# One region for the kernel's front: set-up, memory keys, input projection, low-rank products and memory attention joined to the scan

## The reference, cut to what matters

```python
kv = rms_norm(mem, mem_norm_g) @ w_mem_kv          # mem: 256 x 1024, kv: 256 x 512
k_mem, v_mem = kv halves, 4 heads of 64            # k_mem normalised per head
h = rms_norm(x, norm_mix_g[0])
z = h @ rw_in                                      # 1024 x 2816: r, k, v, wa, g, q_mem
z[..., :2560] += rw_mu * (shift_by_one_token(z) - z)
w = sigmoid(w0 + tanh(wa_1) @ rw_w2);  a = sigmoid(a0 + wa_2 @ rw_a2)   # low-rank products
y = the RWKV-7 recurrence of r, k, v, w, a, 12 heads, in chunks of 64 tokens
mix = (group_norm(y) + bonus) * (sigmoid(g) @ rw_g2)
mem_out = softmax(norm(q_mem) @ norm(k_mem).T / 8) @ v_mem
x = x + concat([mix, mem_out]) @ w_out
```

## Time and profile before

| | us |
|---|---|
| three runs | 2153.62, 2156.22, 2162.27 |
| their median | 2156.22 |
| profiled execution, time | 2156.99 |
| profiled execution, span | 2154.8 |
| PE busy in the span | 1994.3 |
| DVE, ACT, POOL busy | 904.5, 733.1, 227.4 |
| mean granted TensorE clock | 0.948 |

### The profile page before, as it was taken

One profiled execution on the slowest core, in us unless ns is written; L12 is line 12 of the kernel. 1 busy time (PEld: TensorE's weight loads), 2 busy tenths in 40 slices (PEclk: granted clock), 3 DMA queues, 4 the chain that ended last, 5 costly groups with the idle time before them and its releaser, 6 DMA issues. The chain is left out here.

```text
span 2154.8 us, 32963 instructions
## 1 busy us (share of the span) xinstructions
PE 1994.3 (93%) x13832; PEld 1598.5 (74%) x13832; DVE 904.5 (42%) x1331; ACT 733.1 (34%) x1221; POOL 227.4 (11%) x308
## 2 busy tenths in 40 slices
PE   5897798857999999999799989999999999999998
PEld 4585577724788888888676558888888988888887
DVE  3442576443443344443214664534332345333223
ACT  4323444233332133222215664422222344222222
POOL 2000566201000000010012320000031000000000
PEclk8898899977999999999958999999999999999999
DMA  4132000000333223362400001332232212233231
GB/s 158 59 97 86 3 3 4 3 8 0 98 98 98 87 90 98 98 133 85 116 2 1 1 1 61 97 98 89 88 101 95 79 40 85 92 98 93 81 95 64
DMA packets 152708, 149.81 MB, mean 70 GB/s; under 512 B 11612, under 2 KB 150010, under 8 KB 152570
## 3 DMA queue, kind: packets, MB, share of 16 engines
q1 hardware_dynamic: 152112, 147.66, 22.3%
q10 hardware_dynamic: 458, 0.12, 0.0%
HBM read 144.62 MB, written 2.10 MB: 68 GB/s over the span
## 5 line engine op out<-in xcount | busy, mean ns | idle before, releaser
L242 DVE TENSOR_TENSOR weight_low<-weight_ring,weight_high 128x2048 fp32r<-128x2048 f32 (+3 forms) x142 | 302.5, 2131 | 495.3 <-ACT weight_high L233 495.2
L233 ACT CAST weight_high<-weight_ring 128x2048 fp32r<-128x2048 f32 (+3 forms) x142 | 251.4, 1771 | 420.6 <-PE psum L262 419.8
L260 PE MATMUL psum<-tail_operand_high,weight_high 128*128 128x512 f32 (+1 forms) x768 | 292.4, 381 | 6.1 <-DVE tail_operand_low L2695 5.4
L262 PE MATMUL psum<-tail_operand_high,weight_low 128*128 128x512 f32 (+1 forms) x768 | 290.1, 378 | 0.0
L261 PE MATMUL psum<-tail_operand_low,weight_high 128*128 128x512 f32 (+1 forms) x768 | 290.1, 378 | 0.0
L260 PE MATMUL psum<-tail_hidden_high,weight_high 128*128 128x512 f32 (+1 forms) x520 | 183.3, 353 | 2.5 <-DVE tail_hidden_low L3141 2.5
L261 PE MATMUL psum<-tail_hidden_low,weight_high 128*128 128x512 f32 (+1 forms) x520 | 182.8, 351 | 0.0
L262 PE MATMUL psum<-tail_hidden_high,weight_low 128*128 128x512 f32 (+1 forms) x520 | 182.6, 351 | 0.0
L260 PEld LDWEIGHTS psum<-tail_operand_high,weight_high 128*128 128x128 f32 x768 | 145.2, 189 | 37.7 <-DVE tail_operand_low L2695 4.8
L261 PEld LDWEIGHTS psum<-tail_operand_low,weight_high 128*128 128x128 f32 x768 | 145.2, 189 | 29.7 <-issue 0.5
L262 PEld LDWEIGHTS psum<-tail_operand_high,weight_low 128*128 128x128 f32 x768 | 145.2, 189 | 29.4
(11 more groups left out here) (405 smaller groups left out, 3191.0 us busy)
## 6 DMA issues: line engine op xcount, KB each, us to landing
weight_ring<-in_w_ff SPq DMA_DIRECT2D x32, 1024.0 KB, 5.2
weight_ring<-in_ffn_w_gate SPq DMA_DIRECT2D x22, 1024.0 KB, 5.3
weight_ring<-in_ffn_w_up SPq DMA_DIRECT2D x22, 1024.0 KB, 5.4
weight_ring<-in_ffn_w_down SPq DMA_DIRECT2D x16, 768.0 KB, 4.6
weight_ring<-in_rw_in SPq DMA_DIRECT2D x11, 1024.0 KB, 5.3
weight_ring<-in_ffn_w_down SPq DMA_DIRECT2D x16, 640.0 KB, 4.2
weight_ring<-in_attn_w_in SPq DMA_DIRECT2D x9, 1024.0 KB, 5.4
weight_ring<-in_w_out SPq DMA_DIRECT2D x4, 1024.0 KB, 5.3
```

Of the source, the lines that this page charges most:

```text
L233: act.copy(self.w_hi[:, slot, 0:n], self.ring[:, slot, 0:n]).then_inc(self.panel_high, 1)
L242: dve.tensor_tensor(self.w_lo[:, slot, 0:n], self.ring[:, slot, 0:n], self.w_hi[:, slot, 0:n], ALU.subtract).then_inc(self.panel_low, 1)
L260: pe.matmul(out, w_hi, x_hi, start=start, stop=False)
L262: return pe.matmul(out, w_lo, x_hi, start=False, stop=stop)
```

## The change

Set-up, the two statistics, the memory keys, the input projection, the low-rank products, memory attention and the preparation of pair 0 become one function, `front`, in one region, and the scan's main part is emitted into the same region.

- 13 panels in another order: q_mem, then wa and g, then the two memory panels, then r, k and v in turns. `front` multiplies 26 groups (two to a panel), numbered s = 0 to 25, in three PSUM banks in turn. Groups 4 to 7 are the memory's and have 256 columns. Groups 8 to 25 are r, k and v (`first_r` is 8).
- The norms of x and mem are taken by token before the transposes: ACT squares a tile of 128 tokens with an accumulated sum, then logarithm and exponential of one column; DVE scales the tile. The gain is applied as the operand is split out of PSUM, by ACT (`mul`) and DVE. x unscaled is turned once more for the residual, two blocks behind each of the groups 2 to 5.
- Behind the groups stand fillers: memory transposes after 1, head sums of q after 3, of k after 6, low-rank products after 8, 9 and 10, scores after 11, 13, 15 and 17, transposes of the weights after 13, 15, 17 and 19, products with `v_mem` after 14, 16, 18 and 20.
- The preparation of pair 0 is spread over the groups 18 to 24.
- SP issues x, panel 0, seven vectors, mem, panel 1, the other vectors and the low-rank weights, then the panels as slots come free. ACT issues eight vectors. The shifts write the slab directly. The low-rank products take half the rows instead of a weight padded with zeros.
- Memory attention's result goes into the slab's place of q_mem, and ACT copies it into `mix` at the start of `rwkv_out`. The region `memory_attention` is gone.

The core of the diff (the functions of the scan's preparation are moved out of the region's bodies and otherwise the same):

```diff
+FRONT = (("rw", 10), ("rw", 9), ("mem", 0), ("mem", 1)) + tuple(("rw", 3 * n + i) for i in range(3) for n in range(3))
...
+    @block.sync
+    def _(sp):
+        for i in range(TT):
+            sp.dma_start(t.x_in[:, i, :], ins["x"][0, i * P:(i + 1) * P, :]).then_inc(x_landed[i], 16)
+        k.load_panels(sp, 1)
+        for dst, src in rows_a[8:]:
+            sp.dma_start(dst, src).then_inc(rows_landed, 16)
+        for i in range(2):
+            sp.dma_start(t.mem_in[:, i, :], ins["mem"][0, i * P:(i + 1) * P, :]).then_inc(mem_landed[i], 16)
+        k.load_panels(sp, 2)
+        for dst, src in rows_rest:
+            sp.dma_start(dst, src).then_inc(rest_landed, 16)
+        for half, name in enumerate(("rw_w2", "rw_a2")):
+            sp.dma_start(t.low[half * HD:(half + 1) * HD, :], ins[name][0]).then_inc(low_landed, 16)
+        k.load_panels(sp, k.lookahead("front"))
...
+    @block.scalar
...
+        for s, (kind, b) in enumerate(groups):
+            bank = ps[:, s % 3, :]
+            group_done(act, s)
...
+                act.copy(t.z[:, c % 2, 1:T + 1], bank).then_inc(evicted, 1)
+            if s % 2:
+                k.split_high(act, 0, 0, s // 2 + 2)
...
+            if first_r <= s < first_r + 3:
+                rates(2 * (s - first_r), 2 * (s - first_r) + 1)
...
+            if s in turn_at:
...
+                act.copy(t.probs_T, ps[:, 6:8, :]).then_inc(copied, 1)
+            if s in scores_at:
...
+                for q in range(TT):
+                    act.activation(t.probs[:, q, :], ps[:, 4 + q // 2, (q % 2) * M:(q % 2 + 1) * M], ACT.Exp,
...
+            if s == 20:
...
+                scan.square(act, 0)
+                scan.still(act, 0)
+            if s == 21:
+                scan.root(act, 0)
+            if s == 22:
+                scan.decays(act, 0)
...
+    @block.vector
...
+        for s, (kind, b) in enumerate(groups):
+            if s % 2:
+                k.split_low(dve, 0, 0, s // 2 + 2)
...
+                dve.wait_ge(evicted, s + 1)
...
+                dve.tensor_tensor(here, z[:, 0:T], z[:, 1:T + 1], ALU.subtract).then_inc(stepped, 1)
...
+            if s == 21:
+                scan.clip(dve, 0)
+            if s == 22:
+                scan.unit_key(dve, 0)
+            if s == 23:
+                scan.against(dve, 0)
+            if s == 24:
+                scan.bonus(dve, 0)
...
+    @block.tensor
...
+        for s, (kind, b) in enumerate(groups):
+            m = s % 2
+            if m == 0:
+                w_hi, w_lo = k.panel(pe, 0, s // 8, s // 2 % 4, KT, PW)
+            if s >= 3:
+                pe.wait_ge(evicted, s - 2)
...
+            if s == 20:
+                pe.wait_ge(copied, heads)
+                scan.key_norm(pe, 0)
+            if s == 22:
+                scan.bonus_sum(pe, 0)
+        pe.wait_ge(placed, heads)
...
+                act.copy(out[:, PAIRS:KT, :], slab[:, SLAB_Q:SLAB_Q + 2, :])
...
-        memory_attention(k, slab, mix)
```

More of the change, by code:

```diff
@@ L11 @@
+from collections import namedtuple
 from contextlib import ExitStack
@@ L143, in add @@
             self.phases.append((name, n, view, kind))
-        add("mem_kv", 2, columns(ins["w_mem_kv"]))
-        add("rw_in", 11, columns(ins["rw_in"][0]))
+        sources = {"rw": columns(ins["rw_in"][0]), "mem": columns(ins["w_mem_kv"])}
+        add("front", len(FRONT), listed([sources[kind](i) for kind, i in FRONT]), "listed")
         add("w_out", 4, columns(ins["w_out"][0]))
@@ L609, in wait_block @@
-def wait_block(eng, k, g0, made, i, b):
-    if b % 2 == 0:
-        eng.wait_ge(made, 4 * i + b // 2 + 1)
-    else:
-        eng.wait_ge(k.panel_used, 4 * i + (g0 + b // 2 + 1))
-def stream_columns(pe, k, name, x, made, bank_free, need=lambda b: b + 1):
-    g0, ps = k.first_panel[name], k.ps
-    n = next(p[1] for p in k.phases if p[0] == name)
-    def body(i, j):
-        w_hi, w_lo = k.panel(pe, g0, i, j, KT, PW)
-        for m in range(2):
-            pe.wait_ge(bank_free, 8 * i + need(2 * j + m))
-            at = slice(m * P, (m + 1) * P)
-            for kt in range(KT):
-                if isinstance(i, int) and i == j == m == 0:
-                    x.ready(pe, kt)
-                last = product(pe, ps[:, 2 * j + m, :], (w_hi[:, kt, at], w_lo[:, kt, at]), x.halves(kt), kt == 0, kt == KT - 1)
-            last.then_inc(k.panel_used if m else made, 1)
-    in_fours(pe, n, body)
@@ new lines, in vector_rows @@
+def vector_rows(k, t):
+    ins, out_a, out_b, out_pe = k.ins, [], [], []
+    for table, tile, row, out in ((VEC_A, t.vec_a, ROW_A, out_a), (VEC_B, t.vec_b, ROW_B, out_b)):
+        for name, n in table:
+            a = ins[name]
+            if n == 1:
+                out += [(tile[row[name]:row[name] + 1, half * HD:(half + 1) * HD], a) for half in range(2)]
+                continue
+            order = {1: "(r c) -> r c", 2: "l (r c) -> (l r) c", 3: "l n (r c) -> (l n r) c"}
+            if name == "rw_r_k":
+                flat = a.rearrange("l (r h) c -> (l r) (h c)", h=2)
+            else:
+                flat = a.rearrange(order[len(a.shape)], c=P)
+            out.append((tile[row[name]:row[name] + n, :], flat))
+    for kv in range(2):
+        for half in range(2):
+            out_pe.append((t.pe_in[:, kv, half * HD:(half + 1) * HD], ins["nsa_cmp_pe_2"][0, kv]))
+    return out_a, out_b + out_pe
```

1611 lines of the change are left out of this document (793 added, 818 removed).

## The result

| | before | after |
|---|---|---|
| median of the timed runs | 2158.23 us (4 runs, 2153.62 to 2162.27) | 2077.84 us (4 runs, 2073.89 to 2079.68) |
| the profiled execution | 2156.99 us, span 2154.8 | 2079.68 us, span 2077.9 |
| mean granted clock of TensorE | 0.948 | 0.965 |
| ratio | | 0.9632, interval 0.9618 to 0.9646 |

The change takes 80.4 us off the median, 3.7%. The forecast was 2077, in a range of 2063 to 2093.

What follows compares the result with a forecast made beforehand. All stages in one were taken as bound by chains of small work, only the projection by PE. Savings of 50.2 (memory attention) and 33.1 (front), less 3.2 returned, gave 80.1 off 2156.99: 2077 us, range 2063 to 2093.

Steps and rivals of the forecast that it cites:

- wait for the memory's low parts: Groups 1 to 7: the residual's first transposes wait 1.2 us for the low parts, ready 8.7 after group 1.
- head 0 waits: Memory attention's first head inside the groups: PE comes after 13.1, its chain ends at 13.9, wait 0.8 us; others none.
- wait in group 22: PE's `bonus_sum` behind group 22 waits 6.2 us for `rk`, held up by the order of ACT's and DVE's queues.
- slow clock behind it: After the pause in group 22 PE's clock falls; 2.6 us taken, between nothing and 5.6.
- scan's first product: End of the front: the scan's first product starts at 203.7 instead of 236.8, minus 33.1 us.
- scan's first product to pair 0's copy (DVE late): Scan start: group 25's split and shift delay DVE's mask operations; 3.2 us comes back, bounds 0 and 6.
- memory attention gone: Behind the scan: the next stage needs only `mix`, so it starts where memory attention did, minus 50.2 us.
- In the loop itself nothing changes, nor behind it: Scan loop and all stages after it: no change in time, so no term in the sum.
- 1.28 for each 128x1024 operation: Front's start: DVE's scaling of x tiles 2 and 3 at two-input speed, last tile ready at 15.3 us.
- the covered late waits: Rival: ACT evicts group 22 early and DVE is free at scan start; 6.2 + 2.6 + 3.2 fall away, 2065; chance 0.12.
- The heads did not wait: Rival denied here: with 5 us more per chain, all four heads wait 2.4 and restarts cost 2.6, 2097; chance 0.22.
- The low clock in the front: Rival: PE's clock stays low through groups 1 to 25 and fillers, 150 us more, 2227; chance 0.02.

Runs made afterwards that it cites:

- kept busy: The kernel after, with seven unused fp32 products of 512 columns on PE ahead of the preparation's second sum behind group 22; 2077.85 us, ratio 0.9623.
- sum later: The kernel after, with PE issuing the preparation's second sum one group later, behind group 23 instead of 22; 2068.95 us, ratio 0.9592.
- split later: The kernel after, with ACT's and DVE's split of the panel behind the projection's last moved from group 25 to the scan's last pair; 2073.82 us, ratio 0.9610.
- no heads: The kernel after, with memory attention's four heads left out on all engines and the normed queries in their place; 2053.89 us.
- rows first: The kernel after, with the seven small rows issued ahead of the first weight panel on the sync queue; 2075.90 us, ratio 0.9623.

## Why the prediction was right, and where not

Step by step, forecast against the profile of after, and against the means of three profiles of each kernel where they matter:

| step | forecast | profiled pair | means of three |
|---|---|---|---|
| group 0 ends | 25.2 | 24.9 | |
| group 7 ends, evicted | 62.6 | 62.4 | |
| wait for the memory's low parts | 1.2 | 0.6 | |
| head 0 waits | 0.8 | 0.3 | |
| wait in group 22 | 6.2 | 6.9 | |
| slow clock behind it | 2.6 | | 2.7 (kept busy) |
| scan's first product | -33.1 | -34.8 | -32.8 |
| scan's first product to pair 0's copy (DVE late) | +3.2 | +3.1 | +3.6 |
| pair 0's copy to pair 5's copy | 0 | +3.2 | +3.1 |
| pair 5's copy to what follows `rwkv_out` | 0 | -2.9 | -2.0 |
| memory attention gone | -50.2 | -50.2 | -53.6 |
| behind the cast | 0 | +4.7 | +2.8 |
| sum, by the span | -80.1 | -76.9 | -78.9 |

The copy is ACT's into `scan_a_av`, one in each pair. What follows `rwkv_out` is memory attention in before and the cast in after.

The mechanism was right at each place that was named: the groups pass at the full clock, each chain lies under them, one pause stands in group 22, and DVE is late for the scan. Sum later, kept busy, split later and no heads each take one of these terms out and find its size, at the scan's first product or (split later) at the cast, within 1 us of the forecast, but for the heads' 1.9.

That the total came out within 1 us is luck, however: wrong terms of 2 to 3.4 us cancelled. "In the loop itself nothing changes, nor behind it" was costed at exactly zero. True of the instructions, it is wrong of the time at three places. First, the loop. The first and last of the six copies, before and then after:
```profile
248.94 0.62 ACT L897 COPY scan_a_av<-scan_tok 128x512 f32<-128x512 f32 x1
...
400.11 0.62 ACT L897 COPY scan_a_av<-scan_tok 128x512 f32<-128x512 f32 x1
```
```profile
217.18 0.62 ACT L1093 COPY scan_a_av<-scan_tok 128x512 f32<-128x512 f32 x1
...
371.56 0.62 ACT L1093 COPY scan_a_av<-scan_tok 128x512 f32<-128x512 f32 x1
```
That is 151.2 against 154.4; the three profiles of each kernel have 150.8 to 151.2 and 153.5 to 154.4. Second, between the last copy and the end of `rwkv_out`, 2.0 come back. Third, a sparse stage far behind, the pool mixer, took 61 to 67 us, at different granted clocks. And the 50.2 of memory attention was read from one execution, at a clock of 0.67; two others had 0.62 and 0.50 and took 53.0 and 57.6. By the mean of three the part taken out was worth 3.4 more than the row said. The last two should have had bounds of some 5 us of their own; the range had room for them, though nothing in it was set aside.

Of the 4.8 that come back between the scan's first product and the cast, split later shows 3.5, at its start. The loop is no shorter in it (154.4), so the loop's 3.1 have another cause. It is not the clock (1.00 in the loop in both kernels), nor PE's work (135.9 busy against 135.3). It is where PE stands still and waits for nothing that the profile shows ("issue"): between the two copies 2.9 to 3.3 in all in the profiles of before, 5.3 to 5.9 in those of after, by the means 2.6 of the 3.1. One such stop of 1.0, between the first and the second pair's copy, stands in all three profiles of after and in none of before. No heads has 3.5, and a loop of 151.5. Which part of the change makes PE stop there was not tried.

The 2.6 for the slow clock behind the pause fell on its measured 2.7 by luck. It was a value chosen between nothing and 5.6, and the reading behind it was wrong: of the two rows of four passes that it compares, 3.68 "after a pause" and 1.93 "without", each stands behind the same 1.10. They show the two clocks (granted 1.00 from 505.1 to 507.1, 0.50 from 512.3 to 516.0), not what a pause does.

Smaller ones. The wait in group 22 was 0.7 short because DVE's copy for head 3 (0.69) stands ahead of the clip, and I had not counted it in the queue. At the start the rows landed at 12.8, not 12, which the scaling of x made good.

For that scaling I took 1.28 for each 128x1024 operation. DVE's rows of after:
```profile
13.36 1.50 DVE L674 TENSOR_SCALAR rwkv_slab<-rwkv_lw_rate,front_square_sums 128x1024 f32<-128x1024 f32 x2
...
23.90 0.76 DVE L686 TENSOR_SCALAR rwkv_lw_rate<-rwkv_lw_rate,front_square_sums 128x1024 f32<-128x1024 f32 x1 [0.20 <-ACT front_square_sums L563]
```
Two of them take 1.50, one alone 0.76, though the second of all took 1.42 (at 7.94) and the first 0.97. In rows first the two take 1.80. The Trainium skill, "VectorE: DVE Perf Modes", section on mode 2x_2P, with its estimated 0.65, was the nearer guide by this trace; the 1.1 us are in the start's earlier end.

Of the rivals, the covered late waits did not occur by themselves, but sum later and split later are that case made on purpose. The heads did not wait: 0.3 and 0.5. The low clock in the front did not occur; with three banks the window from 62.6 to 175 has a clock of 1.00. So the swinging clock that the Trainium skill, "TensorE: Matmul & The Clock Gate", section on psum-queue depth-cycling, tells of for short pauses between groups is not seen here, where PE pauses 0.9 us in 112.

## What to carry to other kernels

When stages of small chains are merged under a stage that keeps TensorE busy, count every engine's queue by hand around each hand-over: the price left is where one engine's order puts a chain's link behind the group it should overlap, and one group's shift of a single step was worth 8 us here. The pause of 6.9 us cost its length and then about 2.7 us of slow clock behind it. Work with a late use (the split of a panel that nobody needs for 200 us) should not stand ahead of a stage's critical start. And compare landmarks in two traces from a common start rather than totals, and take stages in which TensorE idles often from several executions.

## What the runs showed of the hardware that was not expected

- A stage with many short pauses of TensorE has no single duration. The same instructions of memory attention took 50.2, 53.0 and 57.6 us (granted clock 0.67, 0.62, 0.50), those of the pool mixer 61.2 to 67.1 in 13 profiles. The stages where PE is dense do not vary so: from x to the scan's first product three profiles of after lie within 0.5 us in 183.
- PE stops of about 1 us, in which it waits for nothing that the profile shows, can differ between two kernels that run the same loop: 2.9 to 3.3 us in all between the first and the last pair's copy in before, 5.3 to 5.9 in after, and alike in the profiles of one kernel.
- The landing of x and the small rows shifts the whole program by 1.3 us between executions (first split product at 19.25 to 20.54 in kernels with the same loads).
- One DVE operation can take twice its time at the start of the program: the scaling of x that took 1.42 at 7.94 us took 0.75 later; the cause was not tried.
